# An unused gap in SBUF cut from 112 to 64 words, in a kernel of three transformer layers

## What is computed

```python
# two layers (the second without context output)
h = modulate(rmsnorm(x, g1), ...)          # 512 rows: 256 tokens + 256 context
z = h @ w_in                               # 1024 x 2304
mix = [gated mixing, short convolution, Fourier mixing, differential attention]
x = x + gt1 * (mix @ w_out)                # 1024 x 1024
x = x + gt2 * conv_ffn(h2, w_up, w_down)   # 1024 x 5632, 2816 x 1024
# third layer: mLSTM and window attention, then an expert layer
z = h @ w_in_2; ...; (...) @ w_out_2
q = h @ w_query                            # 1024 x 2048
s = q . sub_keys; top 16 of 128 x 128 experts for each of 8 heads
a = gelu(expert_u[idx] . h); y = sum (softmax * a) * expert_v[idx]
```

## Time and profile before

| | us |
|---|---|
| three runs | 2180.17, 2184.13, 2193.90 |
| median | 2184.13 |
| profiled execution, whole | 2185.96 |
| its span, first to last instruction | 2184.2 |
| PE busy | 2094.0 |
| PEld busy | 1987.5 |
| DVE / ACT / POOL busy | 1436.1 / 1085.3 / 480.6 |

### The profile page before, as it was taken

The page is one execution under the profiler, slowest core; times in us unless marked ns, Lnnn a source line. Parts: engine busy times, 40 slices in busy tenths (PEclk is TensorE's granted clock), DMA queues, the critical chain, the costliest instruction groups (busy, mean ns, idle before and its releaser), DMA issues.

```text
span 2184.2 us, 42595 instructions
## 1 busy us (share of the span) xinstructions
PE 2094.0 (96%) x18040; PEld 1987.5 (91%) x18040; DVE 1436.1 (66%) x2728; ACT 1085.3 (50%) x1879; POOL 480.6 (22%) x226
## 2 busy tenths in 40 slices
PE   7999999999998989999889988999999999999998
PEld 5977999999998789999778888999999999999998
DVE  3445478877785666666663656589388897666665
ACT  5333352232335455546433445555577776555564
POOL 1201100000011120001211341188766662000000
PEclk9999999999998999999999999999999999999999
DMA  7245345566663345654221234555444445555553
GB/s 275 104 139 180 117 164 185 172 223 227 207 222 118 115 145 205 225 196 134 83 70 58 78 109 161 175 193 190 168 140 146 150 146 174 194 193 194 194 194 134
DMA packets 97278, 354.90 MB, mean 162 GB/s; under 512 B 10688, under 2 KB 11712, under 8 KB 96704
## 3 DMA queue, kind: packets, MB, share of 16 engines
q1 hardware_dynamic: 97088, 352.18, 47.9%
HBM read 351.09 MB, written 1.05 MB: 161 GB/s over the span
## 4 chain that ended last, share of the span: by engine, by line
PE 86%; DVE 5%; ACT 3%; issue 3%; DMA 2%; POOL 2%; SPq 0%; ACTq 0%; DVEq 0%; POOLq 0%
PE ps L79 82%; PE ps L84 3%; DVE TL L113 1%; PE ps L106 1%; ACT TH L157 1%; POOL TL L113 1%; DMA RAW<-in_wada 1%; ACT SQ L154 1%; DMA AW<-in_wada 1%; POOL SM L113 0%; ACT Hh L157 0%; DMA RAW<-in_wdn 0%; DVE ps L113 0%; DMA RAW<-in_wup 0%; DVE SQ L113 0%
## 5 line engine op out<-in xcount | busy, mean ns | idle before, releaser
L157 ACT ACTIVATE TH<-RAW 128x1024 fp32r<-128x1024 f32 (+1 forms) x515 | 539.8, 1049 | 281.8 <-PE ps L79 253.6
L113 DVE TENSOR_TENSOR TL<-RAW,TH 128x1024 fp32r<-128x1024 f32 (+1 forms) x343 | 424.5, 1238 | 238.1 <-ACT TH L157 237.2
L113 POOL TENSOR_TENSOR TL<-RAW,TH 128x1024 fp32r<-128x1024 f32 x172 | 413.2, 2405 | 507.2 <-ACT TH L157 481.2
L79 PE MATMUL ps<-Hh,TL 128*128 128x256 f32 x1920 | 450.3, 287 | 17.2 <-DVE TL L113 8.5
L79 PE MATMUL ps<-Hl,TH 128*128 128x256 f32 x1920 | 439.5, 281 | 0.0
L79 PE MATMUL ps<-Hh,TH 128*128 128x256 f32 x1920 | 439.4, 281 | 0.0
L79 PE MATMUL ps<-HXh,TL 128*128 128x256 f32 x1314 | 365.6, 282 | 7.0 <-POOL TL L113 3.1
L79 PEld LDWEIGHTS ps<-Hh,TL 128*128 128x128 f32 x1920 | 322.7, 192 | 42.9 <-issue 17.9
L79 PE MATMUL ps<-HXh,TH 128*128 128x256 f32 x1314 | 360.0, 278 | 0.0
L79 PE MATMUL ps<-HXl,TH 128*128 128x256 f32 x1314 | 359.9, 278 | 0.0
L79 PE MATMUL ps<-W,TH 128*128 128x256 f32 x2052 | 349.1, 276 | 0.0
(11 more groups left out here) (335 smaller groups left out, 3112.4 us busy)
## 6 DMA issues: line engine op xcount, KB each, us to landing
RAW<-in_ut SPq DMA_DIRECT2D x128, 512.0 KB, 3.3
RAW<-in_v SPq DMA_DIRECT2D x128, 512.0 KB, 3.3
RAW<-in_wup SPq DMA_DIRECT2D x88, 512.0 KB, 4.3
AV<-in_wada SPq DMA_DIRECT2D x80, 512.0 KB, 3.8
RAW<-in_win SPq DMA_DIRECT2D x74, 512.0 KB, 3.5
RAW<-in_wada SPq DMA_DIRECT2D x56, 512.0 KB, 3.6
RAW<-in_wdn SPq DMA_DIRECT2D x32, 512.0 KB, 4.4
RAW<-in_wout SPq DMA_DIRECT2D x24, 512.0 KB, 3.7
```

The lines of the kernel that those rows point to most:

```text
L79: return self.e.matmul(out, lhs, rhs, start=first, stop=last, skip_group_check=skip)
L113: return DRY if self.e is None else self.e.tensor_tensor(out, a, b, op)
L157: return DRY if self.e is None else self.e.activation(out, a, ACT.Copy, **kw)
```

## The change

The unused tensor between the split weights and everything behind it is 48 words smaller.

```diff
@@ -445,7 +445,7 @@
     RAW = sb("RAW", NRAW * TILE)
     TH = sb("TH", NSPLIT * TILE, F32R)
     TL = sb("TL", NSPLIT * TILE, F32R)
-    sb("PAD0", 112)
+    sb("PAD0", 64)
     HXh = sb("HXh", 2048, F32R)
     HXl = sb("HXl", 2048, F32R)
     XX = sb("XX", 2048)
```

## The result

| | before | after |
|---|---|---|
| median (runs) | 2184.76 us (4) | 2256.76 us (4) |
| ratio | | 1.0328, interval 1.0291 to 1.0365 |
| profiled execution, whole | 2185.96 | 2261.68 |
| its span | 2184.2 | 2259.9 |

The forecast was 2230 with a range of 2158 to 2240: slower, as it came out, but by 72 us instead of 46. (The median before, 2184.13 from three runs, is 2184.76 with a fourth of 2185.38.)

The account below looks back on a forecast made before the run. The pace of TensorE's wide matmuls was taken to bound the kernel. Slowing the fast ones cost 19.9 + 6.6 + 6.6 + 13.5 = 46.6 us, taken as 46: 2184.13 + 46 = 2230 us, range 2158 to 2240.

Parts of the forecast that it names:

- one relation changes: Start of moving read, counted from start of split weights modulo 512 bytes: 448 before, 256 after; all else stays.
- addresses play no part: Second rival: TensorE's two paces come from how its two queues fall in step; 2184 us, chance 0.18.
- one pace instead of two: Wide matmuls, at 113.3 or 117.9 ns before, would all run at 117.9 ns after.
- I take the slow pace, 117.9 ns, for all wide matmuls: Wide matmuls of mm3: every one at the slower of two traced paces; 46 us more, chance 0.45.
- 4.5 ns for each of 10,375 fast matmuls: Wide matmuls at 113.3 ns, in all stages: each slows by 4.5 ns, in all 46.6 us.
- the signs: Expected profile after: down stage 13.5 us longer, 1,699 records per 200 us instead of 1767, no stretch at 113.3.
- a meeting in the middle: Wide matmuls after: moving read meets the next weight load 57 ns after its start, always paying the slow pace.
- The moving read thus gains one round of 512 bytes: Wide matmuls: moving read streams 1024 bytes, load 512, so they meet about once an interval.
- a meeting near the edge: Wide matmuls before: reads meet 14 ns after the start, so a stream falls into the load or just beside it.
- The first rival: Wide matmuls: a meeting in the middle is absorbed, all streams keep 113.3 ns; 2165 us, chance 0.25.
- The third: Rival for wide matmuls: no meeting costs anything, loads set the pace at 111.5 ns; 2140 us, chance 0.07.
- The fourth, the dear end: Rival: 9 ns more for each fast wide matmul, 4.5 for each slow one, 111 us; 2295 us, chance 0.05.

Follow-up runs that it names:

- e1: Kernel before with 80 words put ahead of RAW and the gap kept at 112 words, so everything moves together: 2187.77 us against 2188.55, ratio 0.999.
- e2: Kernel before with the gap cut to 64 words and 48 words put ahead of W alone, restoring the old relation in the down stage only: 2238.23 us.
- e12: Changed kernel, but each matmul with split weights moves its first column over and over instead of 256 or 128 different ones: 2146.62 us.
- e5: Kernel before with a gap of 48 words instead of 112, relation 192: 2191.65 us.
- e3: Kernel before with no gap words instead of 112, relation 0: 2260.34 us.
- e10: Kernel before with TH and TL in one tensor, blocks beginning four words behind its start, gap still 112 words, relation 464: 2244.97 us.
- e9: Kernel before with a gap of 104 words instead of 112, relation 416: 2236.33 us.

## Where the prediction was right and where it was wrong

**Right: what bounds the kernel.** Nearly all of the change is TensorE's pace; transfers and the busy times of the other engines hardly moved, and stage by stage the times follow from the count of matmuls times the change of pace. Two readings on the way were too smooth, without effect on the sum: one digit of the clock row is an eight, not a nine, and the DMA row has one to seven tenths over the whole kernel, four and five only in most of its last third.

**Right: that one relation changes, and that it counts.** e1 and e2 show it directly. The rival "addresses play no part", drawn from what the Trainium skill's pages "SBUF — State Buffer" (section "SBUF: two separate sides") and "TensorE: Matmul & The Clock Gate" (section "Step-by-step: what each phase is for") state, that only the port pair shared by VectorE and GpSimd causes contention and that TensorE's two read ports are independent, falls: here two reads of TensorE itself cost each other 8.2 ns in 120.0 (e12 against after), and the measurement decides.

**Right: one pace instead of two**, no stretch at 113.3, narrow matmuls without effect. That was luck: the way there was wrong, see below.

**Wrong: the size, and with it the range.** The step was "I take the slow pace, 117.9 ns, for all wide matmuls". The pace after is 120.0. The term, 4.5 ns for each of 10,375 fast matmuls, measured 6.7; the 3,934 matmuls at the slow pace, costed at nothing, paid 2.1 each. With these the same sum gives 77.5 instead of 46.6. (The 3,060 x 4.5 = 13.5 of the signs is a slip: it is 13.8, and 13.5 belongs to the 3,005 at the fast pace; the down stage took 20.2 us more.) I had taken 117.9 because it was a pace that the trace had, and put the next dearer end at 9 ns with a chance of 0.05, outside the range. The lesson of the trace was only that 117.9 is a price that occurs at relation 448; nothing tied it to the middle.

**Wrong: the picture of a meeting in the middle.** Two of its steps failed. "The moving read thus gains one round of 512 bytes": the round is 256 bytes (relation 0 costs what 256 costs, 192 has the paces of 448), so in that picture the reads come to the same place about twice an interval, at any relation. And "a meeting near the edge" is not what makes a place cheap: at 0, where both reads start together, every long stream pays the 120.0 of the changed kernel, and with the weights 16 bytes, even one word, off 448 the fast pace is lost. The forecast had the right sign by luck of the picture: it sent 256 to the middle of a round, while it stands at its edge.

**The first rival**, the slow pace goes away, was the opposite of what happened: the fast one went. The third had a floor near the 111.8 ns that e12 reached, and the wrong relation: of those tried, none reaches it with both reads walking. The fourth, the dear end, put 9 ns on a fast matmul and 4.5 on a slow one; 6.7 and 2.1 were paid, between it and the forecast.

**What stays open.** Why 64 and 192 modulo 256 allow 113.3 ns and nothing tried near them does, whether the places off the steps of 64 bytes cost by the relation or by themselves, why a stream takes one of its paces and not another, and whether a matmul pays for the load beside it or for another. The runs show that both reads take part and that, in steps of 64 bytes, their relation modulo 256 decides which paces can occur; how the memory is divided inside is not shown. No kernel tried that computes the whole products beats the one before: e1 and e5, at the same relation modulo 256, equal it (2187.77 and 2191.65 us), all others are slower.

## What to carry to other kernels

Where TensorE's stream bounds a kernel and each matmul has a weight load beside it, the addresses of moving rows against those of the weights are a parameter, worth 3.3% in this one: print them modulo 256, try a few gaps by 64 bytes, and read the result as starts per 200 us in a stretch without waits, not as busy time. Two paces in one trace for the same instructions, at the same clock, were the sign of it here; but a single pace may be the dearer one, as in the changed kernel. A pace that the trace shows at one setting is no bound for another setting: a price that can't be read must keep its dear end in the range.

## What the runs showed of the hardware that was not expected

- A stream of loads of 128 columns and float32r matmuls of 256 columns, all at the full clock, runs at anything from 113.3 ns (before) to 120.0 (after, e3) or 123.3 ns a matmul (some streams of e10) with the same instructions, by where its two operands lie; with the moving read standing still it runs at 111.8 (e12).
- In steps of 64 bytes the dependence repeats at 256 bytes of a partition: 0 and 256 give 1669 records in 200 us each, 192 and 448 give 1767.
- It is sharp: moving the weights by one word from relation 448 turns 113.3 into 118.3 ns.
- At most places a stream keeps one of two or three paces, nearly always until a wait or narrow matmuls break it: 113.3 or 117.8 at 64 and 192 modulo 256, 117.3 or 118.7 at 416 (e9), 117.8, 118.3 or 123.3 at 464 (e10). At 0 modulo 256 all long streams have the same one.
